# A pooling map folded into the output weight, split weights loaded by the sync queue, and the product of probabilities and values moved behind the next matmul group

## The reference

```python
hn = rmsnorm(h, g_attn_norm)
z = hn @ w_in                       # 1024 -> q 512 | k 128 | v 128 | u 512
q, k = rmsnorm per head (64)        # 8 query heads, 2 key and value heads
a = sliding_window_sink_attention(q, k, v, sinks, rel_bias)   # window 128, blocks of 128
# u in 4 channel groups g of 128: mean over the last 2/4/8/16 tokens minus the token
y = einsum('bsgc,gcd->bsgd', pooled, w_pool)      # one 128x128 map for each group
m = y * pool_scale
h = h + concatenate([a, m]) @ w_out               # w_out: 1024 x 1024
hn = rmsnorm(h, g_ffn_norm)
h = h + (silu(hn @ w_gate) * (hn @ w_up)) @ w_down            # d_ff 2816
h = h + sigmoid(rmsnorm(h, g_ple_norm) @ w_ple_gate) * (p @ w_ple_proj)
```

## Time and profile before

| what | value |
| --- | --- |
| runs | 2053.68 us median of 3 (2050.17 to 2062.04) |
| profiled execution | 2053.4 us, its span 2051.5 us |
| PE busy | 2011.2 us, 98% of the span, 9546 instructions |
| DVE busy | 1372.9 us, 67%, 1920 |
| ACT busy | 899.7 us, 44%, 1460 |
| POOL busy | 406.5 us, 20%, 508 |
| DMA, hardware queue q1 | 212.97 MB, 34.1% of the 16 engines' time |
| DMA, software queue q0 (issued by POOL) | 76.96 MB, 10.8% |
| `w_parts<-w_split` | 88 transfers of 512 KB, 4.8 us median from issue to landing |

### The profile page before, as it was taken

The page is one execution under the profiler, slowest core; times in us unless marked ns, Lnnn a source line. Parts: engine busy times, 40 slices in busy tenths (PEclk is TensorE's granted clock), DMA queues, the critical chain, the costliest instruction groups (busy, mean ns, idle before and its releaser), DMA issues.

```text
span 2051.5 us, 26122 instructions
## 1 busy us (share of the span) xinstructions
PE 2011.2 (98%) x9546; PEld 1663.4 (81%) x9546; DVE 1372.9 (67%) x1920; ACT 899.7 (44%) x1460; POOL 406.5 (20%) x508
## 2 busy tenths in 40 slices
PE   8999999999999999999999999999999999999998
PEld 6887878877788888888888878788888888888877
DVE  4696674767696665655888765966566566987663
ACT  4575754657433333333333543533333333334542
POOL 4454644645410000000000220000000000001310
PEclk9999999999999999999999999999999999999999
DMA  7757566364934223225825128432322328352143
GB/s 193 201 180 245 188 236 219 130 236 131 347 127 130 81 72 103 72 72 171 307 62 165 36 72 223 143 119 67 96 85 72 100 79 292 130 159 78 42 134 103
DMA packets 197387, 292.09 MB, mean 142 GB/s; under 512 B 16139, under 2 KB 118452, under 8 KB 195980
## 3 DMA queue, kind: packets, MB, share of 16 engines
q1 hardware_dynamic: 172672, 212.97, 34.1%
q0 software_dynamic: 22176, 76.96, 10.8%
q10 hardware_dynamic: 2412, 0.50, 0.1%
HBM read 223.25 MB, written 67.51 MB: 142 GB/s over the span
## 4 chain that ended last, share of the span: by engine, by line
PE 84%; DVE 6%; DMA 3%; issue 3%; ACT 2%; POOL 1%; SPq 0%; ACTq 0%; DVEq 0%; POOLq 0%
PE bank L2623 13%; PE bank L2627 13%; PE bank L2625 13%; PE bank L2660 7%; PE bank L2661 7%; PE bank L2662 7%; PE bank L2323 4%; PE bank L2325 4%; PE bank L2324 4%; PE bank L2299 2%; PE bank L2301 2%; PE bank L2300 2%; DMA w_parts<-w_split 1%; PE bank L2392 1%; DVE w_lo L1554 1%
## 5 line engine op out<-in xcount | busy, mean ns | idle before, releaser
L2623 PE MATMUL bank<-a_hi,ring_hi 128*128 128x512 f32 x1232 | 479.7, 389 | 1.0 <-DVE ring_lo L1917 0.7
L2627 PE MATMUL bank<-a_hi,ring_lo 128*128 128x512 f32 x1232 | 479.3, 389 | 0.0
L2625 PE MATMUL bank<-a_lo,ring_hi 128*128 128x512 f32 x1232 | 479.3, 389 | 0.0
L2623 PEld LDWEIGHTS bank<-a_hi,ring_hi 128*128 128x128 f32 x1232 | 231.3, 188 | 49.9 <-DVE ring_lo L1917 1.4
L2625 PEld LDWEIGHTS bank<-a_lo,ring_hi 128*128 128x128 f32 x1232 | 231.3, 188 | 48.0
L2627 PEld LDWEIGHTS bank<-a_hi,ring_lo 128*128 128x128 f32 x1232 | 231.3, 188 | 47.8
L2660 PE MATMUL bank<-d_hi 128*128 128x512 f32 x616 | 239.8, 389 | 0.0
L2662 PE MATMUL bank<-d_hi,d_lo 128*128 128x512 f32 x616 | 239.7, 389 | 0.0
L2661 PE MATMUL bank<-d_lo,d_hi 128*128 128x512 f32 x616 | 239.6, 389 | 0.0
L1376 ACT ACTIVATE d_hi<-keep 128x1024 fp32r<-128x1024 f32 x132 | 139.8, 1061 | 201.9 <-PE bank L2662 184.9
L975 POOL DMA_DIRECT2D hidden_T<-hid x88 | 47.6, 541 | 770.4 <-DVE hid L1953 750.7
(11 more groups left out here) (258 smaller groups left out, 3879.9 us busy)
## 6 DMA issues: line engine op xcount, KB each, us to landing
w_parts<-w_split POOLq DMA_DIRECT2D x88, 512.0 KB, 4.8
hidden_T<-hid POOLq DMA_DIRECT2D x88, 256.0 KB, 2.3
raws<-in_w_gate SPq DMA_DIRECT2D x80, 256.0 KB, 4.7
raws<-in_w_up SPq DMA_DIRECT2D x80, 256.0 KB, 5.1
keep<-hidden_T SPq DMA_DIRECT2D x66, 256.0 KB, 3.8
raw<-in_w_ple_gate SPq DMA_DIRECT2D x64, 256.0 KB, 4.2
keep<-in_w_down SPq DMA_DIRECT2D x44, 256.0 KB, 4.4
other<-hidden_T SPq DMA_DIRECT2D x44, 256.0 KB, 6.8
```

Source lines behind the costliest of these rows:

```text
L2623: mm(dst[:, :], wh[:, g, cols], a_hi[o][:, k, :], start=fresh and k == 0, stop=False, skip_group_check=True)
L2625: mm(dst[:, :], wh[:, g, cols], a_lo[o][:, k, :], start=False, stop=False, skip_group_check=True)
L2627: ins = mm(dst[:, :], wl[:, g, cols], a_hi[o][:, k, :], start=False, stop=k == 3, skip_group_check=True)
```

## The change

It has six parts.

1. The pooling map is folded into the output weight. In section z of tile 0, rows 512 to 1023 of `w_out` are loaded by ACT's queue (`wo_raw`, 4 x 512 KB), scaled by `pool_scale` and split by ACT (`pooled_rows_hi`, half panels 10 to 13) and DVE (`pooled_rows_lo`, 11 to 14), multiplied by `w_pool` on PE (`mix_rows`, 13 to 16, six matmuls of 512 columns for each group), copied out by ACT and stored by POOL as `w_mixed`. The output panels of those rows are loaded from `w_mixed`. `pool_y`, its ACT copy and its DVE rest are gone for all four tiles.
2. The parts are loaded by SP's queue, between its other loads, and these are spaced anew: the x chunks of tile 3 at the end of z(2), the h blocks of tile 1 over two panels, the blocks for the feed-forward part over four.
3. ACT also copies the keys' bank to `k_raw`, DVE subtracts from that and not from the bank, and the transposes of probabilities wait for `kT_hi` and not for `kT_lo`.
4. The product of probabilities and values is put off behind the first group of the next half panel, in 27 of 32 steps.
5. DVE's copy of `u` stands behind the hosted step in some half panels.
6. In the last stages the norm work of the next part (transposes of squares, spread, scaling) comes one panel later.

The core of the diff:

```diff
+            def pooled_rows_hi(g):
+                if g == 0:
+                    act.wait_ge(consts, CONSTS + 16 * NPOOL)
+                nc.scalar.activation(wo_hi[g][:, :], wo_raw[g][:, :], ACT.Copy,
+                                     scale=scale_sb[:, g:g + 1]).then_inc(wp_hi_done, 1)
...
+            def mix_rows(g):
+                pe.wait_ge(wp_lo_done, g + 2)
+                if g == 0:
+                    pe.wait_ge(kvcopied, NB)
+                elif g >= 2:
+                    pe.wait_ge(mixed_copied, 2 * g - 2)
+                for e in range(2):
+                    dst, cols = mixed_bank_of(g, e), slice(e * T, (e + 1) * T)
+                    mm(dst[:, :], wp_hi[:, g, :], wo_hi[g][:, cols], start=True, stop=False)
+                    mm(dst[:, :], wp_hi[:, g, :], wo_lo[g][:, cols], start=False, stop=False)
+                    mm(dst[:, :], wp_lo[:, g, :], wo_hi[g][:, cols], start=False, stop=True
+                       ).then_inc(mixed_bank, 1)
...
-                    if t:
-                        for g in POOL_Z.get(half, ()):
-                            pool_y(t - 1, g)
...
                     if e == 0 and r >= 2 and part == 0:
-                        pe.wait_ge(y_lo, 4 * t + 2 * r - 2)
+                        pe.wait_ge(pool_lo, 4 * t + 2 * r - 2)
...
-                return rows(w_out, 2 * r, 2 * r + 2, cols)
+                return rows(w_mixed[:, :], 2 * r - 4, 2 * r - 2, cols)
...
+            def load_parts(i):
...
+                    sp.wait_ge(panel_used, i - SLOTS_W + 1)
+                sp.wait_ge(parts_stored[kept % 2], 32 * (kept // 2 + 1))
+                for part in range(2):
+                    sp.dma_start(w_parts[parts_slot(i)][:, part, :].bitcast(F32), w_split[kept, part]
+                                   ).then_inc(parts_landed[parts_slot(i)], 16)
...
+                if n:
+                    act.wait_ge(kstaged, n)
+                nc.scalar.activation(k_raw[:, :], bank[5][:, 0:P], ACT.Copy)
                 nc.scalar.activation(kT_hi[:, (b + 1) * P:(b + 2) * P], bank[5][:, 0:P],
                                      ACT.Copy).then_inc(k_hi_done, 1)
...
-                nc.vector.tensor_tensor(kT_lo[:, cols], bank[5][:, 0:P], kT_hi[:, cols].bitcast(F32),
+                nc.vector.tensor_tensor(kT_lo[:, cols], k_raw[:, :], kT_hi[:, cols].bitcast(F32),
...
-                pe.wait_ge(kstaged, 4 * s + min((k + 1) // PAIRS + 1, NB))
+                pe.wait_ge(k_hi_done, 4 * s + min((k + 1) // PAIRS + 1, NB))
...
+            def attends_at_once(s, k):
+                return s in (1, 2) and k in (8, 12) or (s, k) == (2, 18)
...
-                if has_unit(k, LAG_PV):
+                if has_unit(k, LAG_PV) and attends_at_once(s, k):
                     attend(16 * s + k - LAG_PV, (k - LAG_PV) % PAIRS)
...
                     if next_block(k):
                         return lambda: transpose_probs(s, k)
+                    if has_unit(k, LAG_PV) and not attends_at_once(s, k):
+                        return lambda: attend(16 * s + k - LAG_PV, (k - LAG_PV) % PAIRS)
...
-                                if r == 0:
+                                if r == 1:
                                     pe.wait_ge(pp_copied, 8 * g + 4 + 1)
                                     turn_squares(NORM3[g + 1], acc3, bank[BS0[0]])
```

More of the change, by code:

```diff
@@ L756, in _ @@
                         load_chunk(2, 2 * c - 13)
+                    if t == 1 and c == 9:
+                        for k in range(4):
+                            load_chunk(3, k)
                     if t == 2 and c >= 9:
@@ L760, in _ @@
                     load_out(t, c)
[L761 to L765, removed]
+                    if t == 0 and c == 7:
+                        load_parts(Z_AT[2])
+                    if t:
+                        load_parts(OUT_AT[t] + c + 2)
+                    if t == 1 and c < 2:
+                        load_h(1, 2 * c)
+                        load_h(1, 2 * c + 1)
                     if t < 2:
@@ L938, in z_section @@
                         powers(NORM1[1])
+                    if t == 0:
+                        for g in POOLED_STORE_AT.get(half, ()):
+                            store_mixed(g)
+                    if t == 1 and half == 4:
+                        pool.wait_ge(mixed_stored, 16 * NPOOL)
                     if t >= 2:
@@ L1198, in z_section @@
                         nc.scalar.activation(wp_hi[:, :, :], wp_raw[:, :, :], ACT.Copy).then_inc(wp_hi_done, 1)
+                        for g in range(NPOOL):
+                            act.dma_start(wo_raw[g][:, :], w_out[QW + g * P:QW + (g + 1) * P, :]).then_inc(consts, 16)
                     if t == 0 and 8 <= half < 16:
@@ L1835, in z_section @@
                         normalise2(t - 2, SCALE2_AT[half])
-                    for g in U_COPY_AT[t > 0].get(half, ()):
+                    fresh = any(has_unit(k, 0) and k % 2 == 0 for _, k in hosted_steps("z", t, half))
+                    u_first = fresh or half == 19 or not late
+                    for g in U_COPY_AT[t > 0].get(half, ()) if u_first else ():
                         copy_u(t, g)
@@ L2534, in z_section @@
                     if t == 0 and half == 17:
-                        pe.wait_ge(kvcopied, 2)
+                        pe.wait_ge(mixed_copied, 2 * NPOOL)
                         turn_squares(NORM1[1], acc, bank[5])
+                    if t == 0 and half in POOLED_AT:
+                        mix_rows(POOLED_AT[half])
                     hosted("z", t, half)
```

160 lines of the change are left out of this document (70 added, 90 removed).

## The result

The changed kernel took 2094.69 us (median of 4 runs, 2094.19 to 2095.19), beside 2053.27 for the kernel before (median of 4, taken with it). The ratio is 1.0198, 95% interval 1.0181 to 1.0215: 41 us slower. The forecast was 2065 with a range from 2038 to 2077, so the direction was right and the size was not.

A forecast was written before the change was run, and what follows sets the result against it. The prediction took TensorE (PE), 84% of the page's chain, to bound the kernel; its terms summed to +9.1 us on 2053.5, giving 2062.6, raised to +11 for partly absorbed waits: 2065 us, range 2038 to 2077.

The forecast's parts named there:

- -11.2 - 4.8 + 5.9 + 1.0: Pooling map: matmuls removed -11.2, VectorE's rest no longer waited for -4.8, 24 matmuls added +5.9, possible late panel +1.0.
- the parts' -4.0: Parts by the sync queue: PE's 4.0 us of waits for `w_parts` go; ends -4.0 and 0.
- PE's waits of 4.8 us for L1772 go, -4.8: Pooling map: VectorE's rest goes, and PE's waits for it of 3.1 + 1.0 + 0.7 us with it.
- behind them stand the loads of h, stage and a, none of which I find wanted within its own half panel: SP's queue: loads behind its new waits come in time; -4.0 for the parts, +5 if one wait is late.
- Rival 4: SP's queue blocks at a store or `h`; PE waits for parts, 5 x 2 us: 2075, chance 0.05.
- 16 x 0.9 = 14.4: Put-off product, dense steps: PE idles 0.9 us before transposes of probabilities, awaiting ScalarE's scaling, 16 times: +14.4.
- the transposes of queries write bank 6 and wait for VectorE's sum of that product: Put-off product, steps 6 and 10 before new blocks: PE waits 1.6 us at each of eight, +12.8.
- forecast 8.7: Put-off product: PE's old waits at L2405 (4.5) and L2427 (4.2) fall inside the new ones, -8.7.
- of these 1.8 us I take 1.2, three times: Put-off product, steps 14, where VectorE also has squares and norms: the later scaling costs +3.6.
- -2.6: Last stages, transposes of squares one panel later: PE's wait for GpSimd, 2.6 us in two, goes.
- a split panel behind it may be late, up to +1 each time; I take nothing: Last stages: VectorE's scaling and two subtractions in one block might delay a split panel; counted as nothing.
- The first rival: The put-off product costs only its change of work: 2040, or 2032 if old waits go too; chance 0.24.

The follow-up runs named there:

- the mended kernel: Changed kernel with all products at their old place, tile 3's x chunks loaded earlier, ffn_in_T stores moved to panel 3, last stages' norm work as before: 2039.70 us, ratio 0.9943.
- e4: Changed kernel with chunks 4 to 7 of x for tile 3 loaded ahead of the parts that wait for a slot: 2082.80 us, ratio 1.0137.
- e1: Changed kernel with every product back at its old place, the put-off alone undone: 2059.79 us, ratio 1.0029.
- e5: Kernel before the change with only the put-off of the product added, in the same 27 steps: 2091.42 us, ratio 1.0186.
- e10: The mended kernel with the product put off again in steps 6 and 10 alone: 2049.58 us, ratio 0.9983.
- e11: The mended kernel with the product put off in the other 19 of the 27 steps, not in steps 6 and 10: 2067.24 us, ratio 1.0069.
- e9: Changed kernel with ScalarE's order, in steps with a product alone, made scaling, then copy, then share: 2086.07 us, ratio 1.0162.

## Why the prediction was wrong

**The map.** Right as a sum with its neighbour, not by itself. The steps -11.2 - 4.8 + 5.9 + 1.0 and the parts' -4.0 make -13.1; the mended kernel, which has these two and neither the put-off nor the late stages' move, is 12.4 us faster (2052.1 to 2039.7). That the sum fits so well is in part luck, since its split doesn't. Between the two spans lie 13.6 us; PE's waits fell by 3.2 (34.3 to 31.1), where the terms have 7.8, the clock gave 1.7, and some 8.7 are shorter work, where the terms have 5.3. Alone, the map gave 2. The step that PE's waits of 4.8 us for L1772 go, -4.8, fails when the map is changed alone, since `w_parts` was due at the same place.

**The parts by SP.** The step "behind them stand the loads of h, stage and a, none of which I find wanted within its own half panel" failed. The chunks of `stage` were wanted just there. Rival 4 (SP blocks, PE waits at a few panels, 10 us, 0.05) was near and not the same: it had SP blocked at a store or at `h` and PE waiting for parts, where SP was blocked at the parts and PE waited for what the chunks lead to. And it was no rival to the put-off's price but comes on top of it. Measured: 15.1 us for the chunks and the stores together (2059.8 to 2044.7), of which 11.9 are the chunks by e4 (9 to 10 by the estimate above). The 3 to 6 of the stores are what is left; no run has them alone. The code told it: chunk 4 is asked for in panel 3, behind a pair of parts that waits until panel 2 is used, and ACT wants chunk 4 in half panel 6, the first of panel 3. The other side of the step held. The Trainium skill, page "DMA: Bandwidth & Descriptors", section "Issuing engines are not separate DMA queues", says that another issuing engine saves only time of the issue. The pages of the two profiles agree: from issue to landing the median is 4.8 us before and 4.5 after, and yet the waits for `w_parts` are gone, since the parts are asked for earlier.

**The put-off.** The mechanism, its places and the regular size were right: sixteen waits of 0.92 us (14.7; forecast 16 x 0.9 = 14.4). At the eight new blocks the size was near (10.3; forecast 12.8) and its make-up wrong: the queries' transposes were to wait 1.6 us each for `share` and waited 3.0 us in all, while 7.3 us stand at the keys' transposes behind `probsT_lo`. The step "the transposes of queries write bank 6 and wait for VectorE's sum of that product" left out the other path, through the copy. The old waits were absorbed nearly as said: 23.6 + 10.3 - 26.4 = 7.5 (forecast 8.7). Two terms were too small. The steps 14 cost 8.9 us (forecast 3.6, "of these 1.8 us I take 1.2, three times"), in four tiles and not in three, and what I put down to changes of work 5.2 (forecast 2.7). In all 24.8 was forecast, and 34.9 measured (39 on the kernel before).

**The clock.** No term of the sum had it. The changed kernel lost 10.7 us to it and the one before 3.4. All its falls stood behind waits of 2.4 us or more, two of them at steps 14, three at SP's late loads and one in the last stages. It could have been read before: the wait of 1.9 us of the earlier trace rows has a fall behind it too (the window 370 to 375 us has 0.66), and so has the one of 1.3 us near 1206 (0.76).

**Late stages.** -2.6 was forecast and the move cost 5.0. That PE's wait for GpSimd there goes was true (2.6 us, now 0.6), and the wait for `w_lo`, next in the same place, grew by 2 us each. The step "a split panel behind it may be late, up to +1 each time; I take nothing" failed.

**The raw copy.** No gain and no loss, as taken.

Together: forecast +9.1. The terms that moved it are the put-off (+10), SP (+15) and the late stages (+5 + 2.6): 9.1 + 32.7 = 41.8, against 41.4. These are the steps of one path from the mended kernel to the changed one, so they must add up nearly; the sum is no test by itself.

The first rival (the put-off costs nothing but its changes of work, since ScalarE and VectorE have less to do) is ruled out by e1, e5, e10 and e11. Whether a put-off product could pay with VectorE's work at steps 14 moved away was not tried; e9 says only that ScalarE's order isn't enough. The later copy of `u` (part 5) had no term in the sum and was not tried alone.

## What to carry to other kernels

An operation that is moved later frees its successors' buffers later on every path out of it: price each, since the view of waits names only the last, and a mend of that one brings out the next. When loads move into a queue that waits for "panel used", everything behind them in that queue gets that wait too; write down for each when its reader wants it. And a removed wait counts only down to the next releaser at the same instruction.

## What was not expected of the hardware

In the changed kernel PE's clock fell to 1.2 GHz behind six of the seven idle times of 2.4 us and more in mid-kernel, for some 3.4 us each (6.5 near 337), and never behind those of 0.93, so that a long wait can cost 1.7 us more than its length. It is not a fixed limit: falls also stood behind waits of 1.93 and 1.31 us (the kernel before, near 370 and 1206) and of 1.7 (the mended kernel, near 463), but not behind 2.03 and 2.40 (the changed kernel, 166.5 and 1248), and in the run with the chunks early the two of 2.7 and 2.8 us at steps 14 had none. So a profile can win or lose some us by falls that come and go. Two VectorE subtractions of two SBUF operands (`kT_lo`, `mix_lo`) took up to 1.16 and 1.5 us in place of 0.29 and 0.43 in single cases.
